# Second mixing branch of a two-layer block: where the sink's exponential is made and who adds it to the denominator

## The reference, cut to what matters

```
def sink_softmax(s, sink):
    m = jnp.maximum(jnp.max(s, axis=-1, keepdims=True), sink)
    e = jnp.exp(s - m)
    return e / (jnp.sum(e, axis=-1, keepdims=True) + jnp.exp(sink - m))
```

## Time and profile before

| | before |
|---|---|
| median of 3 runs | 3122.43 us |
| profiled execution | 3122.32 us |
| its span | 3120.5 us |
| TensorE busy | 3027.4 us (97%) |
| VectorE busy | 1868.7 us (60%) |
| ScalarE busy | 1252.7 us (40%) |
| GpSimd busy | 304.7 us (10%) |
| branch 1 of layer 0 | about 640 to 900 us |
| branch 1 of layer 1 | about 1425 to 1660 us |

### The profile page before, as it was taken

How to read it: one execution, slowest core, us unless ns; L and a number is a source line. 1 busy time by engine, 2 the same in 40 slices (tenths; PEclk the granted TensorE clock), 3 DMA queues, 4 the chain that set the end, 5 groups by cost and what they waited for, 6 DMA issues and landing times.

```text
span 3120.5 us, 37010 instructions
## 1 busy us (share of the span) xinstructions
PE 3027.4 (97%) x14782; PEld 2395.6 (77%) x14782; DVE 1868.7 (60%) x2959; ACT 1252.7 (40%) x2004; POOL 304.7 (10%) x222
## 2 busy tenths in 40 slices
PE   8999999999999998999999999999999999999998
PEld 4877887877888677767777777788887866788887
DVE  5877775245435667685554786666435685566632
ACT  3344523135432344534454474322225656322222
POOL 0012200001100002202220021000003210000000
PEclk9999999999999999999999999999999989999999
DMA  5222132320012322222112233222332310232332
GB/s 208 69 74 69 54 99 92 110 95 21 28 34 78 105 81 81 68 82 69 51 55 81 75 101 97 88 95 95 97 94 89 115 38 1 84 95 93 94 96 72
DMA packets 78732, 251.50 MB, mean 81 GB/s; under 512 B 9121, under 2 KB 11169, under 8 KB 78561
## 3 DMA queue, kind: packets, MB, share of 16 engines
q1 hardware_dynamic: 72672, 227.91, 22.9%
q0 software_dynamic: 5024, 18.09, 1.8%
q10 hardware_dynamic: 864, 3.15, 0.3%
HBM read 247.01 MB, written 2.10 MB: 80 GB/s over the span
## 4 chain that ended last, share of the span: by engine, by line
PE 47%; ACT 3%; DVE 3%; issue 1%; DMA 0%; DVEq 0%; ACTq 0%
PE PS L1168 32%; PE PS L1806 5%; PE PS L2850 3%; PE PS L2945 1%; PE PS L1930 1%; PE PS L2910 0%; ACT WH L1117 0%; PE PS L2926 0%; PE PS L2872 0%; ACT PS L2993 0%; PE PS L2911 0%; PE PS L2927 0%; ACT PTN L3007 0%; PE PS L2578 0%; PE PS L1910 0%
## 5 line engine op out<-in xcount | busy, mean ns | idle before, releaser
L1127 DVE TENSOR_TENSOR WL<-RAW,WH 128x1024 fp32r<-128x1024 f32 (+3 forms) x374 | 425.1, 1137 | 490.3 <-ACT WH L1117 489.4
L1117 ACT ACTIVATE WH<-RAW 128x1024 fp32r<-128x1024 f32 (+3 forms) x397 | 384.5, 971 | 436.4 <-PE PS L1168 331.0
L1806 PE MATMUL PS<-Hh,WH 128*128 128x512 f32 x1376 | 525.6, 382 | 14.6 <-DVE WL L1127 7.7
L1806 PE MATMUL PS<-Hl,WH 128*128 128x512 f32 x1376 | 487.7, 354 | 0.0
L1806 PE MATMUL PS<-Hh,WL 128*128 128x512 f32 x1376 | 487.4, 354 | 0.0
L1806 PEld LDWEIGHTS PS<-Hh,WH 128*128 128x128 f32 x1376 | 260.5, 189 | 74.3 <-issue 21.6
L1168 PE MATMUL PS<-XH,WH 128*128 128x512 f32 x768 | 305.0, 397 | 0.0
L1168 PE MATMUL PS<-XH,WL 128*128 128x512 f32 x768 | 303.4, 395 | 0.0
L1168 PE MATMUL PS<-XL,WH 128*128 128x512 f32 x768 | 303.3, 395 | 0.0
L1806 PEld LDWEIGHTS PS<-Hl,WH 128*128 128x128 f32 x1376 | 260.9, 190 | 48.3 <-issue 10.1
L1806 PEld LDWEIGHTS PS<-Hh,WL 128*128 128x128 f32 x1376 | 260.8, 190 | 40.2
(11 more groups left out here) (403 smaller groups left out, 5714.9 us busy)
## 6 DMA issues: line engine op xcount, KB each, us to landing
RAW<-in_w_in SPq DMA_DIRECT2D x124, 512.0 KB, 3.6
RAW<-in_ffn_in SPq DMA_DIRECT2D x96, 512.0 KB, 3.6
RAW<-in_ffn_out SPq DMA_DIRECT2D x48, 512.0 KB, 3.5
RAW<-in_w_ada SPq DMA_DIRECT2D x32, 384.0 KB, 3.6
RAW<-in_nsa_in SPq DMA_DIRECT2D x21, 512.0 KB, 3.3
RAW<-in_lru_in SPq DMA_DIRECT2D x20, 512.0 KB, 3.6
MW<-in_w_ada SPq DMA_DIRECT2D x32, 256.0 KB, 9.7
BS<-in_bs POOLq DMA_DIRECT2D x16, 512.0 KB, 3.9
```

What stands on the lines that cost most here:

```text
L1117: act.activation(WH[half[j]][:, 0:n], RAW[j % NRAW][:, 0:n], ACT.Copy).then_inc(*did("act_whi", ("whi", j)))
L1127: dve.tensor_tensor(WL[half[j]][:, 0:n], RAW[j % NRAW][:, 0:n], WH[half[j]][:, 0:n].bitcast(F32), ALU.subtract).then_inc(*did("dve_wlo", ( ...
L1806: mm = pe.matmul(ps[:, c:c + w_], wt[:, 128 * k:128 * k + 128], x[:, a:a + w_], start=(k == 0 and q == 0), stop=(k == n - 1 and q == 2))
```

## The change

The column of maxima is broadcast to 64 columns before it is turned, so that 64 equal rows stand in PSUM. `es` becomes part of `rows` (behind both `tr`) and takes its exponentials from PSUM, on 64 partitions. PSUM banks of `tr` are released by the row's copy and by `es`. The unit `sink` is no longer TensorE's: VectorE adds ER to the 64 rows of denominators. The maxima are written rounded (F32R), and GpSimd's memsets of ER go. The diff, cut to its core:

```diff
         def rows(p, f):
-            return [("tr", L, br, p, f, half) for half in range(2 if L == 0 else 1)]
+            return [("tr", L, br, p, f, half) for half in range(2 if L == 0 else 1)] + ([("es", L, br, p, f)] if br else [])
...
-                if i == 1 and br:
-                    out.append(("es", L, br, p, f))
...
-                B.release(u, ("row",) + u[1:])
+                B.release(u, ("row",) + u[1:], ("es",) + u[1:] if br else None)
...
-                mm = pe.transpose(B.of(u)[0:1, 128 * i:128 * i + 128], NM[:, 32 * f + t_:32 * f + t_ + 1], ident)
+                top = NM[:, 32 * f + t_:32 * f + t_ + 1]
+                if br:
+                    mm = pe.transpose(B.of(u)[0:64, 128 * i:128 * i + 128], top.broadcast_to([128, 64]), ident)
...
-        def pe_sink(pe, L, br, u):
-            p, f = u[3:]
-            pick = CO[:, 192:320] if slot(br, p, f) else CO[:, 256:384]
-            for half, (a0, n, c) in enumerate(RX[L]):
-                for w in due("pe", [("es", L, br, p, f, h) for h in range(2 if L == 0 else 1)], ("co",)):
-                    pe.wait_ge(*w)
-                mm = pe.matmul(out_bank(L, f)[:, a0:a0 + n], pick, ER[L][half][:, 0:n], start=False, stop=True)
-            mm.then_inc(*did("pe_pv", ("sk",) + u[1:]))
...
+        def act_sink(act, L, br, p, f, B):
             for half, (a0, n, c) in enumerate(RX[L]):
-                row = QB[L, br][64:65, f, a0:a0 + n]
-                for w in due("act", ("row", L, br, p, f, half), before):
+                bank = B.of(("tr", L, br, p, f, half))
+                for w in due("act", ("rowt", L, br, p, f, half), ("sk", L, br, p, 0) if f else ("sk", L, br, p - 1, 1) if p else ("attn", L, br)):
                     act.wait_ge(*w)
-                act.activation(ER[L][half][64:65, 0:n], row.bitcast(F32), ACT.Exp, bias=sm(f"sink{L}", 2 * p + f, 1)[64:65, :]).then_inc(*did("act_row", ("es", L, br, p, f, half)))
+                act.activation(ER[L][half][0:64, 0:n], bank[0:64, 0:n], ACT.Exp, bias=sm(f"sink{L}", 2 * p + f, 1)[0:64, :], scale=-1.0).then_inc(*did("act_row", ("es", L, br, p, f, half)))
...
+                elif u[0] == "sink":
+                    p, f = u[3:]
+                    den = sums(L, br, u)[0]
+                    for half, (a0, n, c) in enumerate(RX[L]):
+                        for w in due("dve", ("pv", L, br, p, f, len(score_parts(L, br)) - 1), ("es", L, br, p, f, half)):
+                            dve.wait_ge(*w)
+                        dve.tensor_tensor(den[:, a0:a0 + n], den[:, a0:a0 + n], ER[L][half][0:64, 0:n], ALU.add).then_inc(*did("dve_sk", ("sk", L, br, p, f)))
...
-                dve.scalar_tensor_tensor(mx[:, 0:4], mx[:, 0:4], ...
+                dve.scalar_tensor_tensor(mx[:, 0:4].bitcast(F32R), mx[:, 0:4], ...
...
-            for e in ER[L][0:2 - L] if br else ():
-                pool.memset(e[:, :], 0.0).then_inc(*did("pool_set", ("ez", L)))
```

More of the change, by code:

```diff
@@ L1828, in pe_attn @@
                     pe_mix_values(pe, L, br, u, B)
-                elif u[0] == "sink":
-                    pe_sink(pe, L, br, u)
                 elif u[0] in ("ln1", "lnv"):
@@ L1891, in pe_rows @@
             for i, t_ in enumerate(tiles):
-                mm = pe.transpose(B.of(u)[0:1, 128 * i:128 * i + 128], NM[:, 32 * f + t_:32 * f + t_ + 1], ident)
+                top = NM[:, 32 * f + t_:32 * f + t_ + 1]
+                if br:
+                    mm = pe.transpose(B.of(u)[0:64, 128 * i:128 * i + 128], top.broadcast_to([128, 64]), ident)
+                else:
+                    mm = pe.transpose(B.of(u)[0:1, 128 * i:128 * i + 128], top, ident)
             mm.then_inc(*did("pe_row", ("rowt",) + u[1:]))
@@ L1928, in pe_mix_values @@
                 first = i == 0 if ctx_q else k == 0
-                end = (i == 1 if ctx_q else k == last and i == len(parts[k]) - 1) and not br
+                end = i == 1 if ctx_q else k == last and i == len(parts[k]) - 1
                 mm = pe.matmul(dst, VV[L, br][:, b, 64 * g:64 * g + 128], src, start=first, stop=end)
             mm.then_inc(*did("pe_pv", ("pv",) + u[1:]))
-        def pe_sink(pe, L, br, u):
-            p, f = u[3:]
-            pick = CO[:, 192:320] if slot(br, p, f) else CO[:, 256:384]
-            for half, (a0, n, c) in enumerate(RX[L]):
-                for w in due("pe", [("es", L, br, p, f, h) for h in range(2 if L == 0 else 1)], ("co",)):
-                    pe.wait_ge(*w)
-                mm = pe.matmul(out_bank(L, f)[:, a0:a0 + n], pick, ER[L][half][:, 0:n], start=False, stop=True)
-            mm.then_inc(*did("pe_pv", ("sk",) + u[1:]))
         def act_set(act, L, br):
@@ L2015, in act_attn @@
                 elif u[0] == "es":
-                    act_sink(act, L, br, u)
+                    act_sink(act, L, br, u[3], u[4], B)
                 elif u[0] == "fin":
@@ L2085, in act_rows @@
             act.activation(row, B.of(u)[0:1, 0:n], ACT.Copy, scale=-1.0).then_inc(*did("act_row", ("row",) + u[1:]))
-        def act_sink(act, L, br, u):
-            p, f = u[3:]
-            before = ("sk", L, br, p, 0) if f else ("sk", L, br, p - 1, 1) if p else ("ez", L)
+        def act_sink(act, L, br, p, f, B):
             for half, (a0, n, c) in enumerate(RX[L]):
-                row = QB[L, br][64:65, f, a0:a0 + n]
-                for w in due("act", ("row", L, br, p, f, half), before):
+                bank = B.of(("tr", L, br, p, f, half))
+                for w in due("act", ("rowt", L, br, p, f, half), ("sk", L, br, p, 0) if f else ("sk", L, br, p - 1, 1) if p else ("attn", L, br)):
                     act.wait_ge(*w)
-                act.activation(ER[L][half][64:65, 0:n], row.bitcast(F32), ACT.Exp, bias=sm(f"sink{L}", 2 * p + f, 1)[64:65, :]).then_inc(*did("act_row", ("es", L, br, p, f, half)))
+                act.activation(ER[L][half][0:64, 0:n], bank[0:64, 0:n], ACT.Exp, bias=sm(f"sink{L}", 2 * p + f, 1)[0:64, :], scale=-1.0).then_inc(*did("act_row", ("es", L, br, p, f, half)))
         def sums(L, br, u):
@@ L2245, in dve_max @@
                     dve.wait_ge(*w)
-                dve.scalar_tensor_tensor(mx[:, 0:4], mx[:, 0:4], sm(f"sink{L}", 2 * p + f, 1), mx[:, 8:12], ALU.max, ALU.max).then_inc(*did("dve_mx", ("mxs", L, br, p, f, 0)))
+                dve.scalar_tensor_tensor(mx[:, 0:4].bitcast(F32R), mx[:, 0:4], sm(f"sink{L}", 2 * p + f, 1), mx[:, 8:12], ALU.max, ALU.max).then_inc(*did("dve_mx", ("mxs", L, br, p, f, 0)))
             elif t_ == 4:
@@ L2251, in dve_max @@
                         dve.wait_ge(*w)
-                    dve.tensor_scalar(mx[:, 4:6], mx[:, 4:6], sm(f"sink{L}", 2 * p + f, 1), None, ALU.max).then_inc(*did("dve_mx", ("mxs", L, br, p, f, 1)))
+                    dve.tensor_scalar(mx[:, 4:6].bitcast(F32R), mx[:, 4:6], sm(f"sink{L}", 2 * p + f, 1), None, ALU.max).then_inc(*did("dve_mx", ("mxs", L, br, p, f, 1)))
             else:
```

## The result

The changed kernel takes 3131.98 us (median of 7 runs, 3130.79 to 3137.5) against 3121.81 us (7 runs, 3120.46 to 3123.71) for the kernel before on the same chip: ratio 1.0034, 95% interval [1.0024, 1.0044]. It is 10 us slower. The forecast was 3125 us in a range of 3111 to 3134, with the most chance on "within 0.2%"; the time lies inside the range and over the line. The profiled execution took 3130.79 us (3122.32 before), so the traces differ by 8.5 us.

The account below looks back on a forecast made before the run. TensorE was taken as nearly full, with short VectorE and ScalarE chains limiting what it saves. Layer 0's +4.2 us and layer 1's -1.65 gave +2.5 on 3122.43: 3125 us, own range 3118 to 3130, 8-in-10 range 3111 to 3134.

Parts of the forecast that it names:

- What leaves TensorE: 17.1 us: Both layers' branches: removing the sink matmuls frees 1.29 us a head in layer 0 and 0.85 in layer 1, eight heads each.
- ScalarE and VectorE: 1.1 and 0.7 us: Each head's sink exponentials, and likewise VectorE's new adds, take 1.1 us in layer 0 and 0.7 us in layer 1.
- Head 0.0 of layer 0: +5.8: The add behind `nrm3` delays TensorE's next projection by 2.9 us, and the lowered clock behind the gap costs 2.9 more.
- Heads 0.1, 1.1, 2.1: -0.3 each, and 1.0, 2.0: +0.3 each: Layer 0: ScalarE's extra work takes back most of the saving at the first three; later rotations outweigh it at the others.
- The end of layer 0, head 3.1: 0: Through quotient and gate to the next projection, the add takes as long as the sink matmul did: 0 us.
- Heads 3.0 and 3.1 of layer 1: -1.65: Layer 1's last two heads keep the whole saving of the removed matmul, -0.8 and -0.85 us.
- Clock: TensorE gaps of 1 to 2 us leave its clock alone; a gap near 3.03 us halves it, costing 2.9 us.
- A: Rival: TensorE stays the bound everywhere, so the full 17.1 us are gained, 3105 us; 8 in 100.
- B: Rival: only head 0.0 of layer 0 pays, -10.0 us in all, 3112 us; 14 in 100.
- C: Rival: waits at rotations of heads 1.0 and 2.0 in both layers also lower the clock, 3131 to 3136 us; 18 in 100.
- D: Rival: 64-column broadcasts double each transpose's time on TensorE, at most +10.9 us; counted within C's 18 in 100.
- The own test: Sign: if TensorE's gaps in the two branches, clock included, do not grow by some 15 us, the forecast errs towards A.

Follow-up runs that it names:

- four-pass: The kernel before's F32 sink matmul on TensorE; the kernel before with only the sink's exponentials moved behind both rows took 3129.0 us.
- one-pass sink: Kernel before with TensorE's sink matmul as F32R from one partition: 3115.79 us; with the exponentials also moved behind both rows: 3121.78 us.
- prompt adds: Changed kernel, with VectorE taking every head's adds directly behind that head's last product with the values: 3117.72 us.
- the adds in the old place: Kernel before in its old order, with VectorE adds (of zero rows) replacing TensorE's sink: 3130.84 us.
- short adds: Changed kernel with adds of 8 columns in place of 512 and 256, waits and order kept: 3119.96 us.

## Why the prediction was in the range, and which step failed

The way was forecast rightly, by 2.5 us where 10.2 were measured. The range held because it was wide, and not because the sum was good. In the traces two misses add up: less left TensorE than the 17.1 us (13.0, a miss of 4.1), and more came back as gaps and clock than the 19.6 that the sum implies (23.1, a miss of 3.5). Together they make the two branches 10.1 us longer instead of 2.5.

- **What leaves TensorE: 17.1 us.** Without a sink the kernel is 13.8 us faster, and TensorE's own work in the two branches fell by 13.0 us from the trace of before to that of after, 4.1 less than the term. The sink itself was priced nearly right: by the same sums, TensorE's own work in the two branches is 16 us less without a sink than before (gaps grow by 3.3 us, which leaves about the 13.8). What no term held is that the new order costs TensorE itself some 2 to 3 us: without adds it does 1.7 us more work in the new order than in the old, and with the four-pass and the one-pass sink 3.0 and 2.7 us more. Why is not shown. The one-pass sink is likewise shorter by 1.29 - 0.65 = 0.64 us a head in layer 0 (710.78 - 709.90 - 0.23 = 0.65) and 0.51 in layer 1, 9.2 us in all, and gave 6.4.
- **Wider transposes: 0.** Right: six take 0.82 us, as in the earlier trace rows.

```profile
738.45 0.82 PE L1890 MATMUL PS<-CO,STAT 128*64 128x128 f32 x6
```

- **ScalarE and VectorE: 1.1 and 0.7 us.** Right. The adds' medians are 0.700 and 0.424 us, back to back 714.43 - 713.34 = 1.09. `es` takes 0.682 and 0.457.

```profile
L2154 DVE TENSOR_TENSOR PS<-PS,Ea x16: 683/700/710, 713.3 to 1654.3; 64x512 f32<-64x512 f32 x16
L2154 DVE TENSOR_TENSOR PS<-PS,Eb x8: 414/424/437, 714.0 to 895.6; 64x256 f32<-64x256 f32 x8
```

- **Head 0.0 of layer 0: +5.8.** The mechanism is right, and the size came out by two misses that cancel. The changed kernel comes to the branch 1.7 us early and reaches the next projection 2.1 us late, so +3.8 where I had 2.9 (0.74 us of it is a wait of the first scores for `es`, which I did not list), and the clock costs 1.7 where I had 2.9: +5.5. That the branch could then lose 23 us by the adds was not in it, and the run with the add ahead of `nrm3` shows that some 2.5 us of this chain can be won back, not the 10.
- **Heads 0.1, 1.1, 2.1: -0.3 each, and 1.0, 2.0: +0.3 each. This step failed.** From one pair's first transposes to the next pair's, these should have cancelled. They cost +1.2 us (738.45 to 794.89, against 736.22 to 791.44 before) and +2.4 us (to 852.69, against 846.86; 1.7 us of it is the clock behind the gaps at 802.61 and 804.75). I counted only the 1.1 us of `es` against ScalarE's idle time and left out that ScalarE's logarithm now waits for VectorE's queue, in which the next head's maxima stand ahead. I had named that queue and priced it only for head 0.0. The prompt adds showed the size of that queue: 14.3 us over the kernel, head 0.0, these heads and those of layer 1 together.
- **The end of layer 0, head 3.1: 0.** It cost +1.1 us: a gap of 1.31 us before the next projection in place of 0.19. The profile names no releaser for it. It is there with prompt adds too (1.31) and not without adds (0.19), so it comes with the add and not with its place in the queue.
- **Heads 3.0 and 3.1 of layer 1: -1.65. This failed too.** They cost +2.7 us: 0.3 from the transposes of 3.0 to those of 3.1, 2.4 from there to the output projection (1639.80 to 1677.19, against 1633.69 to 1668.63). I wrote that no chain stands beside them. But the row copy of 3.1 is queued on ScalarE behind the logarithm of 3.0, which waits for the add:

```profile
1638.74 0.59 ACT L2097 ACTIVATE O<-PS 64x512 f32<-64x512 f32 x1 [3.82 <-DVE PS L2154]
...
1642.54 0.58 ACT L2076 ACTIVATE QB<-PS 1x512 fp32r<-1x512 f32 x1
```

```profile
1643.18 0.50 PE L1910 MATMUL PS<-QA,KA 128*128 128x512 f32 x1 [1.38 <-ACT QB L2076]
```

With prompt adds the last gap is 0.20 us. The other heads of layer 1 came out near their terms only in sum (+0.1 us from the transposes of 0.0 to those of 3.0, where 0 was forecast); one by one the steps changed by -0.9 to +1.3 us.

- **Clock.** Gaps of 1 to 2 us were to leave it alone, from the one of 1.36 us before. Most did. One of 1.38 us did not, nor did 0.69 and 1.02 us within 3 us; 1.7 us each. The same pair of 0.69 and 1.02 us one phase earlier left it at 1.00, and so did the pair at the same place in the run with head 0.0's adds ahead of `nrm3`.
- **Rivals.** A is refuted by the result and by the runs that undo one side each: the kernel waits. B had the wrong sign at the other heads. C comes nearest by its number: its time (3131) is the one measured, and the clock costs 5.1 us more in the two branches. But that is luck. None of the three new falls is at the rotations that C named: one is head 0.0's, which the forecast had, two are behind gaps far under 3.03 us at other places, and without any of them the kernel would still be slower. What C describes does happen in the run with the adds in the old place, at heads 1.0 and 2.0 of layer 1. D is out.
- **The own test:** gaps and clock were to grow by some 15 us. They grew by 12.6 + 5.4 + 3.4 + 1.7 = 23.1 us, against 13.0 of work removed. The 15 did not follow from the forecast, whose +2.5 us with 17.1 removed ask for 19.6; the miss by that is 3.5 us.

## What to carry to other kernels

When a step moves to another engine, price its place in that engine's queue as well as its length. The adds of sixteen heads cost 23 us in one place and 9 in another, up to 4.5 us earlier. Behind reductions that were not urgent, they kept another engine's whole queue waiting. Do this at every place where the step occurs, not only where the chain is plain. A fixed order shared by all engines can be bent for one of them, and both ends of that bend are read in the profile: who idles before the consumer, and which bank the postponed work holds.

## What the runs showed of the hardware

**The clock does not follow from a gap's length alone.** At the same place of layer 1, gaps of 3.01, 3.03 and 3.02 us left the granted clock at 1.00 (2.4 GHz) in three profiled executions, without a sink, with short adds and with prompt adds, where the earlier trace rows have 0.52 behind 3.03 us. The first of the three, its gap and the stretches behind it:

```profile
1459.16 0.45 PE L1875 MATMUL PS<-KA,QA 128*128 128x384 f32 x1 [3.01 <-DVE STAT L2243]
```

```profile
1459.00:1462.00 3.00, 2.84 (x18) 2.57 (x19) 2.42 (x5) 0.00 (x0) 0.00 (x0) 1.00 0.22 73
1462.00:1465.00 3.00, 3.00 (x17) 2.32 (x16) 1.64 (x4) 1.74 (x3) 0.00 (x0) 1.00 0.00 0
```

A fall costs 1.7 to 3.4 us here. Later in the program, where no edit reaches, the falls at about 2500 us cost 1.7 us in the profiled execution with prompt adds, 5.1 in that of before and 6.8 in that without a sink. By their size such differences can make the 8 us between the kernel before's own runs; that they do is not shown, since only one run of each kernel was profiled.

**VectorE and GpSimd slow each other.** In the changed kernel the late quotient pushes GpSimd's gate over VectorE's weight split (the changed kernel first, then the one with prompt adds):

```profile
799.96 1.84 POOL L2315 TENSOR_TENSOR O<-O,T 64x768 f32<-64x768 f32 x1 [10.78 <-DVE O L2264]
800.51 2.37 DVE L1125 TENSOR_TENSOR WL<-RAW,WH 128x1024 fp32r<-128x1024 f32 x1 [0.63 <-ACT WH L1115]
801.96 1.61 POOL L2293 CAST QB<-T 64x768 fp32r<-64x768 f32 x1 [0.16 <-POOL O L2315]
803.70 0.95 DVE L2226 TENSOR_TENSOR QA<-T,QB 64x768 fp32r<-64x768 f32 x1 [0.82 <-POOL QB L2293]
804.75 0.46 PE L1873 MATMUL PS<-KA,QA 128*128 128x256 f32 x1 [1.02 <-DVE QA L2226]
```

```profile
796.62 1.85 POOL L2319 TENSOR_TENSOR O<-O,T 64x768 f32<-64x768 f32 x1 [8.86 <-DVE O L2268]
798.63 0.82 POOL L2297 CAST QB<-T 64x768 fp32r<-64x768 f32 x1 [0.16 <-POOL O L2319]
799.17 1.36 DVE L1125 TENSOR_TENSOR WL<-RAW,WH 128x1024 fp32r<-128x1024 f32 x1 [2.63 <-ACT WH L1115]
```

The split takes 2.37 us beside the gate and 1.36 where it meets only the last 0.28 us of the cast (1.21 at 1642.09 us, with GpSimd idle); the cast takes 1.61 beside the split and 0.82 where it is nearly alone. VectorE's `out` operation (line 2226) waits 0.82 us for the cast, and TensorE's 1.02 us wait for that operation. The Trainium skill, page "SBUF — State Buffer", section "SBUF: two separate sides", says that a VectorE operation with two SBUF inputs and a GpSimd operation that reads SBUF shut each other out for a whole instruction. The rows agree: the split ends 1.08 us after the gate (802.88 against 801.80), the cast 0.69 us after the split (803.57). This is a second way in which a late add costs more than its length; how much of the 23 us it makes was not measured.

**Matmul types.** 512 columns of the sink take 0.85 us as F32 from 128 partitions and 0.34 us as F32R from one partition; no run tells the type's share from that of the partitions. Broadcasting the operand of the transposes to 64 columns raises the median weight load from 83 to 110 ns, while six of them take 0.82 us as before.
